# A third feature pair of a down projection in seven block products, its four extra banks kept as rows over three quarters

## What is computed

```python
h = h + rms_norm(m @ w_o[l], g_post_mix[l])
u = rms_norm(h, g_pre_mlp[l])
f = jnp.square(jax.nn.relu(u @ w_up[l])) @ w_down[l]      # 2048 -> 8192 -> 2048
h = h + rms_norm(f, g_post_mlp[l])
```

## Time and profile before

| | us |
|---|---|
| median of 3 runs (2041.61 to 2042.46) | 2041.9 |
| the profiled execution, by the same clock | 2042.42 |
| its span, first to last instruction | 2040.6 |
| PE busy in the span | 2027.5 |
| DVE busy | 1442.1 |
| ACT busy | 970.1 |
| mean granted TensorE clock, of full speed | 0.999 |

### The profile page before, as it was taken

How to read it: one execution, slowest core, us unless ns; L and a number is a source line. 1 busy time by engine, 2 the same in 40 slices (tenths; PEclk the granted TensorE clock), 3 DMA queues, 4 the chain that set the end, 5 groups by cost and what they waited for, 6 DMA issues and landing times.

```text
span 2040.6 us, 28978 instructions
## 1 busy us (share of the span) xinstructions
PE 2027.5 (99%) x10536; PEld 1724.7 (85%) x10536; DVE 1442.1 (71%) x1945; ACT 970.1 (48%) x1255; POOL 80.7 (4%) x91
## 2 busy tenths in 40 slices
PE   9999999999999999999999999999999999999998
PEld 7888898888888888999888888888888888888886
DVE  6766766566756565678999856577767877877655
ACT  6645444565544444433444644553443443444343
POOL 0000102001001000002000000000000000000001
PEclk9999999999999999999999999999999999999999
DMA  9687656656677666555666676645675565566663
GB/s 349 195 202 186 178 156 178 182 167 180 186 216 229 187 187 187 175 175 157 190 192 201 180 234 187 206 149 173 196 222 180 183 213 184 165 205 207 194 194 105
DMA packets 265476, 389.33 MB, mean 191 GB/s; under 512 B 12505, under 2 KB 147033, under 8 KB 264572
## 3 DMA queue, kind: packets, MB, share of 16 engines
q1 hardware_dynamic: 262587, 377.19, 61.3%
q0 software_dynamic: 2624, 10.54, 1.9%
q10 hardware_dynamic: 144, 0.01, 0.0%
HBM read 385.02 MB, written 2.54 MB: 190 GB/s over the span
## 4 chain that ended last, share of the span: by engine, by line
PE 96%; DVE 2%; SPq 1%; DMA 1%; ACT 0%; issue 0%; DVEq 0%; ACTq 0%
PE acc L700 18%; PE acc L677 18%; PE acc L679 17%; PE acc L678 17%; PE acc L698 10%; PE acc L692 2%; PE acc L690 2%; PE acc L691 2%; PE acc L696 1%; PE aux L1602 1%; DVE low_rows L531 1%; PE aux L1686 1%; PE aux L725 1%; PE aux L727 1%; PE aux L726 1%; DMA stage_rows<-in_w_mem_kv 1%
## 5 line engine op out<-in xcount | busy, mean ns | idle before, releaser
L531 DVE TENSOR_TENSOR low_rows<-stage_rows,high_rows 128x1024 fp32r<-128x1024 f32 x462 | 560.8, 1222 | 335.0 <-ACT high_rows L517 328.7
L517 ACT ACTIVATE high_rows<-stage_rows 128x1024 fp32r<-128x1024 f32 x462 | 481.2, 1047 | 554.3 <-PE acc L679 496.6
L517 ACT ACTIVATE w_high<-stage 128x1024 fp32r<-128x1024 f32 (+1 forms) x264 | 276.3, 1047 | 417.1 <-PE acc L700 298.9
L531 DVE TENSOR_TENSOR w_low<-stage,w_high 128x1024 fp32r<-128x1024 f32 (+1 forms) x264 | 320.8, 1221 | 211.6 <-ACT w_high L517 206.3
L700 PE MATMUL acc<-u,w_high 128*128 128x512 f32 x900 | 248.0, 394 | 0.0
L700 PE MATMUL acc<-hT,w_high 128*128 128x512 f32 x645 | 177.5, 394 | 0.0
L700 PEld LDWEIGHTS acc<-u,w_high 128*128 128x128 f32 x900 | 152.9, 189 | 19.1
L698 PEld LDWEIGHTS acc<-u,w_low 128*128 128x128 f32 x960 | 146.8, 188 | 20.5
L677 PE MATMUL acc<-high_rows,f_pair 128*128 128x512 f32 x400 | 156.4, 391 | 1.4 <-DVEq L2568 1.3
L679 PE MATMUL acc<-high_rows,f_pair 128*128 128x512 f32 x400 | 155.7, 389 | 0.0
L678 PE MATMUL acc<-low_rows,f_pair 128*128 128x512 f32 x400 | 155.7, 389 | 0.0
(11 more groups left out here) (454 smaller groups left out, 3498.4 us busy)
## 6 DMA issues: line engine op xcount, KB each, us to landing
stage_rows<-in_w_in SPq DMA_DIRECT2D x160, 512.0 KB, 3.9
stage<-in_w_in SPq DMA_DIRECT2D x136, 512.0 KB, 3.7
stage_rows<-in_w_down SPq DMA_DIRECT2D x128, 512.0 KB, 4.4
stage<-in_w_up SPq DMA_DIRECT2D x120, 512.0 KB, 4.1
stage_rows<-in_w_o SPq DMA_DIRECT2D x64, 512.0 KB, 4.2
stage_rows<-in_w_pool_out SPq DMA_DIRECT2D x16, 512.0 KB, 4.3
stage_rows<-in_w_conv_out SPq DMA_DIRECT2D x16, 512.0 KB, 4.7
stage_rows<-in_w_mem_kv SPq DMA_DIRECT2D x14, 512.0 KB, 11.4
```

Of the source, the lines that this page charges most:

```text
L517: act.activation(high[:, pr, k_from:kt, 0:p.cols], src[:, slot, k_from:kt, 0:p.cols], ACT.Copy).then_inc(high_done, 1)
L531: dve.tensor_tensor(low[:, pr, k_from:kt, 0:p.cols], src[:, slot, k_from:kt, 0:p.cols], high[:, pr, k_from:kt, 0:p.cols].bitcast(F32), ALU ...
```

## The change

`SEVENS` becomes (2, 4, 6): three pairs of each quarter 0 to 2 in seven products. A step has 22 slabs: 0, 1 pair 0; 2 to 5 the seven of pair 2; 6, 7 pair 1; 8 to 11 the seven of pair 4; 12, 13 pair 3; 14 to 17 the seven of pair 6; 18 to 21 pairs 5 and 7. `f_sums` grows to three pairs.

The banks `aux` are no longer spread in each step. In q = 0 ACT copies all four to SBUF rows (`z_rows`, beside slabs 17 and 19), in q = 1 and 2 DVE adds them to these rows (two beside slab 17, two beside slab 18), and one `z_spread` of 16 DVE operations is done beside eight slabs of `w_up3`. In q = 0 the body of `w_down` copies its banks where it added them. `gain_rows` moves in memory, and its load to the start of `w_up3`; the body of `w_o_2` waits for the load of `mix_gain` alone. Where LEFT lies in the last place of the ring, the blocks of the sums are named the other way round (`turned`).

```diff
-SEVENS = (2, 5)
-SEVEN_ORDER = ((0,), (2,), (1,), (3,), (5,), (4,), (6, 7))
+SEVENS = (2, 4, 6)
+SEVEN_ORDER = ((0,), (2,), (1,), (4,), (3,), (6,), (5, 7))
...
-        gain_rows = at("gain_rows", Z + 40, [P, D])
+        gain_rows = at("gain_rows", Z + 32, [P, D])
...
-        f_raw = at("f_raw", Z + 80, [P, 4, P])
-        seven_u = at("seven_u", Z + 116, [P, ROW])
-        seven_v = at("seven_v", Z + 118, [P, ROW])
-        seven_w = at("seven_w", Z + 120, [P, ROW])
+        f_raw = at("f_raw", 72.25, [P, 4, P])
+        z_at = ((Z + 44, Z + 46, Z + 80, Z + 82), (Z + 116, Z + 118, Z + 120, 80.75))
+        z_rows = [[at(f"z_rows{step}{b}", kb, [P, ROW]) for b, kb in enumerate(places)] for step, places in enumerate(z_at)]
...
+        SPREAD_AT = (5, 8, 11, 14, 17, 20, 23, 26)
...
+                ends = stage_tiles[:, left:left + 4:3, :] if left < right else stage_tiles[:, right + 1:left + 1:left - right - 1, :]
+                dve.tensor_tensor(stage_tiles[:, outer:outer + 2, :], ends,
...
                     if kind == LEFT:
                         n = job.slab0 + step * job.S + idx
-                        assert n % STAGES < STAGES - 1
                         SUMS_BEFORE.update({n - 2: (OUTER, n), n - 1: ("first_inner", n), n: (INNER, n)})
         stage_tiles = stage_rows[:].rearrange("p s k n -> p (s k) n")
 
@@ -538,12 +537,13 @@
                 slab_landed(dve, n)
                 slab_landed(dve, n + 1)
                 dve.wait_ge(split_done, n + 2 + 1)
-                dve.tensor_tensor(stage_tiles[:, outer:outer + 2, :], stage_tiles[:, left:left + 4:3, :],
+                ends = stage_tiles[:, left:left + 4:3, :] if left < right else stage_tiles[:, right + 1:left + 1:left - right - 1, :]
+                dve.tensor_tensor(stage_tiles[:, outer:outer + 2, :], ends,
                                   stage_tiles[:, right:right + 1, :].to_broadcast([P, 2, ROW]), ALU.add).then_inc(landed[(n + 2) % STAGES], 16)
             elif kind == "first_inner":
                 slab_landed(dve, n + 2)
                 dve.wait_ge(split_done, n + 3 + 1)
-                dve.tensor_tensor(stage_tiles[:, inner, :], stage_tiles[:, outer, :], stage_tiles[:, right + 1, :], ALU.add).then_inc(s("inner_sum"), 1)
+                dve.tensor_tensor(stage_tiles[:, inner, :], stage_tiles[:, outer if left < right else outer + 1, :], stage_tiles[:, right + 1, :], ALU.add).then_inc(s("inner_sum"), 1)
             else:
                 dve.wait_ge(s("inner_sum"), 1 + sevens_before(n))
                 dve.tensor_tensor(stage_tiles[:, inner + 1, :], stage_tiles[:, inner, :], stage_tiles[:, left + 1, :], ALU.add).then_inc(landed[(n + 3) % STAGES], 16)
@@ -706,19 +706,23 @@
 
             p, _, k0, _, _ = job.pieces[idx]
             kind, pr, pair = job.kinds[idx], n % PAIRS, k0 // 2
+            turned = 1 if (n - 2) % STAGES == STAGES - 1 else 0
             e, step = SEVENS.index(pair), int(job.name[-1]) * job.steps + i * job.unroll + u
             (_, one, _), (_, two, _) = (job.group(i, u, part) for part in range(2))
             if kind == LEFT:
                 pe.wait_ge(s("f_sums_ready"), len(SEVENS) * int(job.name[-1]) + e + 1)
                 if e == 0 and step:
-                    pe.wait_ge(s("sevens_out"), step)
+                    if step <= 2:
+                        pe.wait_ge(s("z_copied"), 4 * step)
+                    else:
+                        pe.wait_ge(s("z_summed"), 4 * (step - 2))
...
             pool.dma_start(mix_gain[:], A["g_post_mix_2"].partition_broadcast(P)).then_inc(s("gains_in"), 16)
+            pool.wait_ge(s("gains_in"), 16)
+            pool.wait_ge(used, PAIRS + jobs["w_up3"].slab0)
             pool.dma_start(gain_rows[:], A["g_post_mlp_2"].partition_broadcast(P)).then_inc(s("gains_in"), 16)
...
-            def z1_out(q):
+            def copy_z(q):
                 job = jobs[f"w_down{q}"]
                 inner = max(idx for idx, kind in enumerate(job.kinds) if kind == INNER)
 
                 def beside(n):
                     step, idx = n // job.S, n % job.S
-                    if idx == inner:
-                        if q * job.steps + step:
-                            act.wait_ge(s("sevens_out"), q * job.steps + step)
-                        act.wait_ge(used, PAIRS + job.slab0 + n + 1)
-                        act.activation(seven_u[:] if q else y_rows[:, 0, 2 * step * ROW:(2 * step + 1) * ROW], aux[:, 0, :], ACT.Copy).then_inc(s("z1_out"), 1)
+                    for b in {inner: (0, 1), inner + 2: (2, 3)}.get(idx, ()):
+                        act.wait_ge(used, PAIRS + job.slab0 + step * job.S + inner + 1)
+                        act.activation(z_rows[step][b][:], aux[:, b, :], ACT.Copy).then_inc(s("z_copied"), 1)
                 return beside
 
             for q in range(4):
                 rounding(f"w_up{q}", beside=beside_up0 if q == 0 else None)
-                rounding(f"w_down{q}", last_down if q == 3 else None, beside=z1_out(q) if q < 3 else None)
+                rounding(f"w_down{q}", last_down if q == 3 else None, beside=copy_z(q) if q == 0 else None)
...
-                    dve.wait_ge(s("gains_in"), 32)
+                    dve.wait_ge(s("gains_in"), 16)
...
-                    if job.sevens:
-                        dve.wait_ge(dve_link, link.n)
                     for t in range(2):
                         v = y_rows[:, t, r * ROW:(r + 1) * ROW]
-                        dve.tensor_tensor(v, banks[:, t, :], v, ALU.add).then_inc(s("down"), 1)
+                        if q == 0:
+                            dve.tensor_copy(v, banks[:, t, :]).then_inc(s("down"), 1)
+                        else:
+                            dve.tensor_tensor(v, banks[:, t, :], v, ALU.add).then_inc(s("down"), 1)
...
-            def sevens_out(q):
+            def z_spread(step, stage):
+
+                z1, z5, z6, z7 = z_rows[step]
+                y11, y21, y12, y22 = (y_rows[:, t, (2 * step + half) * ROW:(2 * step + half + 1) * ROW] for half in range(2) for t in range(2))
+                if stage == 0:
+                    link(dve.tensor_tensor(y11, y11, z1[:], ALU.add))
+                    link(dve.tensor_tensor(z6[:], z1[:], z6[:], ALU.subtract))
+                elif stage == 1:
+                    link(dve.tensor_tensor(z7[:], z6[:], z7[:], ALU.add))
+                    link(dve.tensor_tensor(z6[:], z6[:], z5[:], ALU.add))
+                elif stage == 2:
+                    link(dve.tensor_tensor(z5[:], z7[:], z5[:], ALU.add))
+                    link(dve.tensor_tensor(y12, y12, z6[:], ALU.subtract))
+                else:
+                    link(dve.tensor_tensor(y21, y21, z7[:], ALU.add))
+                    link(dve.tensor_tensor(y22, y22, z5[:], ALU.subtract))
+
+            def sum_z(q):
                 job = jobs[f"w_down{q}"]
-                z1, z5, z6, z7 = (aux[:, b, :] for b in range(4))
                 inner = max(idx for idx, kind in enumerate(job.kinds) if kind == INNER)
 
                 def beside(n):
                     step, idx = n // job.S, n % job.S
-                    y11, y21, y12, y22 = (y_rows[:, t, (2 * step + half) * ROW:(2 * step + half + 1) * ROW] for half in range(2) for t in range(2))
-                    if idx == inner:
-                        dve.wait_ge(used, PAIRS + job.slab0 + n + 1)
-                        dve.wait_ge(s("z1_out"), q * job.steps + step + 1)
-                        if q:
-                            link.put(dve.tensor_tensor(y11, z1, y11, ALU.add))
-                        link(dve.tensor_tensor(seven_u[:], seven_u[:] if q else y11, z6, ALU.subtract))
-                    if idx == inner + 1:
-                        if q == 0:
-                            link.put(dve.scalar_tensor_tensor(out=y12, in0=seven_u[:], scalar=-1.0, in1=z5, op0=ALU.mult, op1=ALU.subtract))
-                            link(dve.tensor_tensor(y21, seven_u[:], z7, ALU.add))
-                            link(dve.scalar_tensor_tensor(out=y22, in0=y21, scalar=-1.0, in1=z5, op0=ALU.mult, op1=ALU.subtract))
-                        else:
-                            link.put(dve.tensor_tensor(seven_w[:], seven_u[:], z5, ALU.add))
-                            link(dve.tensor_tensor(seven_v[:], seven_u[:], z7, ALU.add))
-                            link.put(dve.tensor_tensor(y12, y12, seven_w[:], ALU.subtract))
-                    if idx == inner + 3:
-                        if q:
-                            link.put(dve.tensor_tensor(y21, y21, seven_v[:], ALU.add))
-                            link(dve.tensor_tensor(seven_v[:], seven_v[:], z5, ALU.add))
-                            link(dve.tensor_tensor(y22, y22, seven_v[:], ALU.subtract))
-                        dve.sem_inc(s("sevens_out"), 1)
+                    for b in {inner: (0, 1), inner + 1: (2, 3)}.get(idx, ()):
+                        if idx == inner and b == 0:
+                            dve.wait_ge(used, PAIRS + job.slab0 + n + 1)
```

(22 more changed lines are left out.)

## The result

| | before | changed |
|---|---|---|
| median of 13 runs, us | 2041.90 | 2046.38 |
| lowest and highest | 2041.57 to 2043.13 | 2045.85 to 2047.60 |
| the profiled execution | 2042.42 | 2045.85 |
| its span | 2040.6 | 2044.1 |

The account below looks back on a forecast made before the run. PE was taken to bound the kernel (busy 99%), with DVE's local slack in `w_down` deciding its stops. Terms -4.08 + 4.3 + 3.5 - 0.6 = +3.1 us gave 2045.0 us against the median of 2041.9, range 2043.5 to 2047.8.

Parts of the forecast that it names:

- What is removed: PE in the down projections: one more seven in 6 steps drops 18 matmuls at 0.2267 us, 4.08 us less.
- The feature sums late in `w_up`: Pair 6's sums delay the fold of group 7, so PE waits at slab 1 of `w_down`: +1.44 us, three times.
- The sum behind a seven: Behind sevens of pairs 2 and 4, DVE's next weight sum delays the following low part: +0.29 us, twelve times.
- T + 4.85: Forecast end of the low part behind a seven, T being when PE starts that seven's LEFT.
- The step's end: PE's stop at slab 1 of second steps in `w_down` shrinks: -0.6 us in all.
- T + 18.84: Forecast end of DVE's last addition at the step's end, T being the start of the third seven.
- What costs nothing: The spread in `w_up3` (11.7 us of DVE) and the late load of `gain_rows` cost PE no time.
- The first: Rival: places behind the sevens cost nothing because DVE's sum starts earlier; 2041.5 us, chance 0.10.
- The second: Rival: both stalls are absorbed and the change brings what it removes; 2037.2 us, chance 0.06.
- The third: Rival: the sum for pair 6's seven waits for its RIGHT slab to land; 2048.6 us, chance 0.17.
- The fourth: Rival: the spread or the load of the gains is not covered; 2046 to 2056 us, chance 0.05.

Follow-up runs that it names:

- e6: Changed kernel with pair 5 for pair 6, first weight sum one slab earlier for second and third sevens, extra-bank additions one at a time: 2037.30 us, 0.9975 of before.
- e3: Changed kernel with only two pairs (2 and 5) in seven products, keeping the kept rows, single spread and late gains load: 2040.86 us, 0.9993 of before.
- e1: Changed kernel with pair 5 instead of pair 6 as the third in seven products: 2041.92 us, 0.9998 of the kernel before.
- e4: Changed kernel without PE's wait for the features at the ordinary slabs of pairs 1 and 3: 2045.51 us, 1.0016 of the kernel before.
- e5: Changed kernel with the first weight sum one slab earlier for only the second and third seven of a step: 2042.49 us, 1.0000 of before.
- e2: Changed kernel with the first weight sum of every seven made one slab earlier: 2041.38 us, 0.9994 of the kernel before.

## Why the prediction was right

**What is removed.** 18 matmuls at the spacing of 0.2267, 4.08 us. Right: e6, which has 366 matmuls a stage and no stops beyond those of e3 (1.97 against 1.99 us), is 5.3 us shorter than before in these stages, 4.1 of it the matmuls. The lengths of the stages show the price without assuming it: the three last 254.96 us together in e3 and 250.85 in e6, so 18 matmuls less are 4.11 us less, 0.228 each. A price of 0.131, which the Trainium skill has for 512 columns in a stream (TensorE: Matmul & The Clock Gate, section Back-to-back issue gap), would leave 1.7 us of it unexplained.

**The feature sums late in `w_up`.** Right. Forecast +1.44 three times, measured 5.12 - 0.85 = 4.27, so 1.42 each. e1 shows the cause: the same operations in group 5 cost nothing.

**The sum behind a seven.** Place and mechanism right (T + 4.85 to the hundredth), size off: 0.35 instead of 0.29, 4.2 in all against 3.5. The term that was mis-sized is the 0.05 us from the low part's end to PE. I took it from a slab with one wait; this one has two, and it took 0.15. e4 shows it by taking one away. So a stop was 0.23 us long and not 0.14, with 0.12 and not 0.15 of refill behind it. This is 0.7 of the 1.4 us that the forecast was short.

**The step's end.** Forecast -0.6, measured 1.96 - 2.31 = -0.35. The working for q = 1 and 2 gives T + 18.84 for the end of the last addition, but the pieces that it names add up to T + 18.6. The rest is a wait of DVE for its own additions ahead of the third weight sum, which the text leaves out (0.21 us in the changed kernel); the trace has the end at T + 18.78. In q = 1 it was 0.67 (forecast 0.74), in q = 0 0.34 (0.25): there the copy out of PSUM took as long as the add, 0.68 us, not the 0.6 that I took. The row of the group (count, busy us and mean ns, idle before):

```profile
L2569 DVE COPY y_rows<-acc 128x512 f32<-128x512 f32 x8 | 5.1, 683 | 0.0
```

The rule of the Trainium skill for fp32 operands in PSUM (VectorE: DVE Perf Modes, section Why PSUM operands drop a tier) was the better guide, and this copy agrees with it: 0.683 us, against 0.43 for one out of SBUF. In q = 2 it was 0.95, 0.28 more than in q = 1 with the same list of work. There ACT began one rounding late. The same place of `w_down1`, then that of `w_down2`:

```profile
1625.90 1.06 ACT L516 ACTIVATE high_rows<-stage_rows 128x1024 fp32r<-128x1024 f32 x1 [0.30 <-PE acc L731]
...
1802.66 1.06 ACT L516 ACTIVATE high_rows<-stage_rows 128x1024 fp32r<-128x1024 f32 x1 [0.58 <-PE acc L731]
```

The idle time is 0.58 where the same place of `w_down1` has 0.30. DVE runs from there to the step's end with no wait for ACT, so PE gets all of it. In e1, e4 and e5 the same rounding begins late by the same amount, and their second steps there lose as much. In e6 it is late too, and that step loses 0.36: spread out, the additions leave DVE the time. What holds ACT stays open: PE had released it at the usual moment, the slab had landed before, and no run was made for it.

**What costs nothing.** Right: `w_up3` is 89.7 us as before with 10.6 us more of DVE in it, and e3 shows it by itself.

**The rivals.** The first (no stop behind the sevens) did not happen: the list of DVE does fix the place. The second (both stalls absorbed, 2037.2 us) did not happen either; its time is what e6 reached, 2037.3, once both causes were moved away. The third (late weights) did not decide in the changed kernel, though its mechanism is real. Landings there were 3.5 to 7.4 us:

```profile
DMA to landing us min/median/max: 3.5/4.3/7.4
```

and none made PE wait. With the sums asked for earlier it depends on the place: in e5 no wait for a landing reached PE, in e2 the waits of 1.08 to 1.58 us did at three places. The fourth fell with e3.

The sum of the terms that I forecast for these stages was +3.1, they came to +4.06: 0.7 from the second wait, 0.25 from the step's end. The other 0.4 of the difference lie between runs, outside these stages.

## What to carry to other kernels

Where one engine is always busy and others feed it through a short ring, a change of the algorithm saves only what the feeding engines' lists allow: place each added operation into a pause that the timeline shows (where DVE waits for ACT), not merely near its use, and check that its inputs have landed by then (e2). Cost each stop at its length plus the refill, from the spacing of starts: busy shares hid the stops, and the list of waits named none of the 12 short ones. When work is added on a feeding engine, look first at what is queued behind it that frees a buffer.

## What the runs showed of the hardware

- Every stop of PE, of 0.13 to 1.57 us, cost 0.12 to 0.15 us beyond its length, until matmuls again started 0.2267 apart.
- From the end of a DVE operation to PE took 0.06 us where PE waited for it alone, and 0.15 where its instruction list had a second wait, already met, at the same slab (e4 against the changed kernel).
- DVE operations in a row without a wait started 1.14 us apart at 1024 elements, although each is reported at 1.22, and 0.61 apart at 512, reported at 0.69.
- Once or twice from 1355 us on, ACT began a rounding about 0.28 us later than usual after PE had released it (idle 0.58 where 0.30 is usual). It was once in `w_down2` of every kernel with three pairs in seven products, at the same slab each time; twice in e3, in `w_down0` and `w_down2`; and in the kernel before once in `w_down1` and once in `w_down3`. It cost PE time in `w_down2` of the changed kernel, e1, e4 and e5; in e2 it cannot be told apart from the waits for landings there, and elsewhere no stop grew by it. The cause is left open.
- An early weight sum waited up to 1.58 us for the landing of its slab, at landings of 3.5 to 6.5 us from issue (e2).
